# A two-block transformer layer on one core: the first norm's row, the order of the first projections, and the layout of their first weights are changed

## What is computed

```
h = rmsnorm(x, g_mix)                       # x: 256 x 1024
z = h @ w_in                                # w_in: 1024 x 2560
b_gate, c_gate, x_in, u, v = split(z)       # 512 columns each
zz   = c_gate * x_in
conv = sum(shift(zz, k) * w_conv[k] for k in range(3))
y_conv = b_gate * conv
y_sgu  = gelu(u) * (w_spatial @ layernorm(gelu(v)) + b_spatial)
x = x + concat(y_conv, y_sgu) @ w_out
x = x + moe(rmsnorm(x))                     # 32 experts, 201 MB of weights
...                                         # gate, second block
```

## Time and profile before

| | before |
|---|---|
| median of 3 runs | 949.59 us (949.17 to 949.7) |
| the profiled execution's own time | 947.69 us |
| its span | 946.0 us |
| TensorE busy in the span | 915.5 us, 97% |
| VectorE, ScalarE, GpSimd busy | 53%, 35%, 4% |
| read from HBM | 287.43 MB, 305 GB/s over the span |
| GB/s in slices 7 to 21 of 40 (142 to 497 us) | 429 to 432 |
| mean granted clock of TensorE | 0.997 |

### The profile page before, as it was taken

One profiled execution on the slowest core, in us unless ns is written; L12 is line 12 of the kernel. 1 busy time (PEld: TensorE's weight loads), 2 busy tenths in 40 slices (PEclk: granted clock), 3 DMA queues, 4 the chain that ended last, 5 costly groups with the idle time before them and its releaser, 6 DMA issues.

```text
span 946.0 us, 14147 instructions
## 1 busy us (share of the span) xinstructions
PE 915.5 (97%) x5866; PEld 647.2 (68%) x5866; DVE 503.3 (53%) x871; ACT 331.1 (35%) x531; POOL 36.7 (4%) x39
## 2 busy tenths in 40 slices
PE   7999999999999899999999989999999999999997
PEld 6997734443344434335453389989989999999886
DVE  7784612222232312123221189999999977766642
ACT  6832210100111000011000088556676755544541
POOL 1000000000000000000000000123320000000000
PEclk9999999999999999999999999999999999999999
DMA  9997799999999999999999984643424435554301
GB/s 345 400 387 311 301 389 430 430 432 430 430 429 430 429 429 430 430 430 429 432 430 421 420 382 159 250 164 142 176 93 178 179 112 198 230 196 179 134 0 45
DMA packets 28981, 289.45 MB, mean 306 GB/s; under 512 B 3056, under 2 KB 6384, under 8 KB 12400
## 3 DMA queue, kind: packets, MB, share of 16 engines
q1 hardware_dynamic: 28192, 286.91, 74.2%
q10 hardware_dynamic: 720, 1.57, 0.4%
HBM read 287.43 MB, written 1.05 MB: 305 GB/s over the span
## 4 chain that ended last, share of the span: by engine, by line
PE 76%; DVE 12%; SPq 5%; ACT 2%; issue 2%; DMA 2%; DVEq 0%; POOL 0%; ACTq 0%
PE ps L279 75%; DVE wl L275 5%; SPq L2325 5%; DMA ring<-in_w_pg 2%; DVE arena L1578 1%; ACT wh L268 1%; PE ps L1081 1%; DMA arena<-in_xT 0%; DVE arena L393 0%; DVE arena L1970 0%; DVE arena L2041 0%; ACT h_h L1449 0%; DVE arena L1486 0%; DVE mg_l L1977 0%; DVE mix_l L624 0%
## 5 line engine op out<-in xcount | busy, mean ns | idle before, releaser
L279 PE MATMUL ps<-ring,arena 128*64 128x512 f32 x1216 | 339.1, 597 | 4.9 <-issue 4.8
L275 DVE TENSOR_TENSOR wl<-ring,wh 128x1024 fp32r<-128x1024 f32 x150 | 182.1, 1247 | 38.3 <-ACT wh L268 38.1
L279 PEld LDWEIGHTS ps<-ring,arena 128*64 128x64 f32 x1216 | 108.9, 137 | 122.6 <-issue 120.9
L268 ACT ACTIVATE wh<-ring 128x1024 fp32r<-128x1024 f32 x150 | 151.9, 1052 | 46.3 <-PE ps L279 30.8
L279 PE MATMUL ps<-arena 128*64 128x512 f32 (+4 forms) x448 | 157.5, 521 | 1.1 <-DMA ring<-in_moe 0.6
L1186 DVE SCALAR_TENSOR_TENSOR arena<-ps,arena 128x512 f32<-128x512 f32 x16 | 12.0, 751 | 202.5 <-PE ps L279 202.5
L279 PEld LDWEIGHTS ps<-arena 128*64 128x64 f32 (+2 forms) x448 | 55.0, 144 | 87.5 <-issue 82.6
L279 PE MATMUL ps<-up_h,wh 128*128 128x256 f32 x352 | 85.5, 281 | 1.1 <-ACT up_h L2030 1.1
L279 PE MATMUL ps<-up_l,wh 128*128 128x256 f32 x352 | 82.1, 280 | 0.0
L1256 ACT ACTIVATE y_h<-ps 128x512 fp32r<-128x512 f32 x32 | 19.0, 596 | 151.9 <-PE ps L279 151.9
L279 PEld LDWEIGHTS ps<-up_h,wh 128*128 128x128 f32 x352 | 66.3, 188 | 1.3 <-issue 1.3
(11 more groups left out here) (283 smaller groups left out, 1460.9 us busy)
## 6 DMA issues: line engine op xcount, KB each, us to landing
ring<-in_moe SPq DMA_DIRECT2D x69, 2048.0 KB, 22.6
arena<-in_moe SPq DMA_DIRECT2D x17, 2048.0 KB, 22.6
ring<-in_w_in SPq DMA_DIRECT2D x12, 2048.0 KB, 9.6
ring<-in_w_up SPq DMA_DIRECT2D x11, 2048.0 KB, 7.9
ring<-in_moe SPq DMA_DIRECT2D x24, 512.0 KB, 15.1
ring<-in_w_dn SPq DMA_DIRECT2D x5, 2048.0 KB, 7.8
ring<-in_w_out SPq DMA_DIRECT2D x4, 2048.0 KB, 16.1
arena<-in_moe SPq DMA_DIRECT2D x8, 512.0 KB, 14.6
```

What stands on the lines that cost most here:

```text
L268: e.activation(wh(i), raw_piece(i), ACT.Copy).then_inc(*hi.up(i))
L275: e.tensor_tensor(wl(i), raw_piece(i), wh(i), SUB).then_inc(*lo.up(i))
L279: return e.matmul(o, l, r, start=first, stop=final, skip_group_check=True)
```

## The change

Five things change together, all in the first projection:

1. The order of the five weights becomes 0, 2, 1, 3, 4: the gate c comes second, v third.
2. The first weight lies in memory piece by piece, so that each of its loads reads one contiguous stretch per partition and not eight of 512 bytes.
3. The row no longer comes from squares by feature. The column `RT` is put on the diagonal of two 128x128 matrices (`DG`), and one product with a matrix of ones spreads it over all partitions. It is placed before the fourth piece of the gate, and the constants are loaded earlier for it (`cst`, which holds the identity).
4. VectorE instead of ScalarE rounds features 4 to 7 of the input. GpSimd has no squares left.
5. Everything that follows is put in an order that fits: on VectorE the gate is scaled ahead of v's mean, and v's variance moves into the convolution's loop.

```diff
-    out = [("in1", i) for i in range(5)] + [("out1", i) for i in range(2)]
+    out = [("in1", i) for i in (0, 2, 1, 3, 4)] + [("out1", i) for i in range(2)]
...
         def mixer_pe(e):
...
-            e.wait_ge(*made.at("ones"))
-            squares((1, 0, 3, 2, 5, 7, 4, 6))
             three(e, ps[3][:, 0:256], "in1", 0, 0, XGH, XGL, xg)
             for j in range(1, 4):
                 three(e, ps[3 + j][:, 0:256], "in1", 0, j, XGH, XGL)
+            for j in range(4):
+                if j == 3:
+                    e.wait_ge(*made.at("ones"))
+                    e.wait_ge(*diag.at(0))
+                    mm(e, ps[7][:, 0:256], one, DG.rearrange("p a b -> p (a b)"), True, True).then_inc(*means.up("r1"))
+                    e.wait_ge(*row.at("r"))
+                three(e, ps[CB[j]][:, 0:256], "in1", 2, j, XGH, XGL)
             for i in range(2):
+                e.wait_ge(*cgate.at(i))
                 wide(e, ps[i][:, :], "in1", 1, i, XGH, XGL)
-            for j in range(4):
-                b = CB[j]
-                if j < 2:
-                    e.wait_ge(*gelu_v.at(j))
-                elif j == 2:
-                    e.wait_ge(*roots.at("r1"))
-                three(e, ps[b][:, 0:256], "in1", 2, j, XGH, XGL)
...
         def mixer_dve(e):
...
+                if c == 4:
+                    for d in range(4, 8):
+                        e.tensor_scalar(XGH[:, d, :], XT[:, d, :], vcol("g_mix", d), None, M).then_inc(*xg_hv.up(d))
...
-            split_lo(e, 4)
-            recip(e, "r1", R1B)
-            e.wait_ge(*recips.at("r1"))
-            e.tensor_tensor(R2B, R1B, R1B, M).then_inc(*vc.up())
+            split_lo(e, 8)
+            recip(e, "rt", RT)
+            e.wait_ge(l_cst, 16)
+            e.wait_ge(*recips.at("rt"))
+            for i in range(2):
+                k = e.tensor_scalar(DG[:, i, :], ident, RT[:, i:i + 1], None, M)
+            k.then_inc(*diag.up(0))
+            e.wait_ge(*means.at("r1"))
+            e.tensor_copy(R1B, ps[7][:, 0:256]).then_inc(*row.up("r"))
+            e.wait_ge(*row.at("r"))
+            e.tensor_tensor(R2B, R1B, R1B, M).then_inc(*row.up("r2"))
             for j in range(4):
                 e.wait_ge(*proj.at("in1", 0, j))
                 e.tensor_tensor(UG[:, j, :], ps[3 + j][:, 0:256], R1B, M).then_inc(*u_.up(j))
-                split_lo(e, j + 6)
-            recip(e, "rt", RT)
-            split_lo(e, 12)
+                split_lo(e, 9 if j else 0)
+            e.wait_ge(*row.at("r2"))
+            for j in range(4):
+                e.wait_ge(*proj.at("in1", 2, j))
+                e.tensor_tensor(CR[:, j, :], ps[CB[j]][:, 0:256], R2B, M).then_inc(*cgate.up(j))
+                split_lo(e, 10 + j)
+            split_lo(e, 14)
             e.wait_ge(*gelu_v.at(1))
...
-            split_lo(e, 14)
+            split_lo(e, 16)
             for j in range(4):
...
-                split_lo(e, j + 20)
+                split_lo(e, j + 18)
             split_lo(e, 24)
...
         def mixer_act(e):
...
-            split_hi(e, 4)
+            split_hi(e, 8)
...
-            root(e, "r1", R1B, ps[2][:, 0:256])
-            split_hi(e, 8)
...
         def loads(e):
...
                 elif i == 0:
-                    dst, src = (v.rearrange("p (c n) -> p c n", c=8) for v in (dst, src))
-                    e.dma_start(dst[:, :, 0:128], src[:, :, 0:128]).then_inc(ring_sem[k], 16)
...
+                    e.dma_start(dst[:, 0:1024], src[:, 0:1024]).then_inc(ring_sem[k], 16)
...
                 if i == 1:
                     e.dma_start(XK, dr["x"]).then_inc(l_xk, 16)
+                    e.dma_start(cst[:], dr["cst"]).then_inc(l_cst, 16)
```

More of the change, by code:

```diff
@@ L178, in build @@
         FIRST = n_piece[("pgate", 0), 0]
-        P = ([("in1", 0, j) for j in range(4)] + [("in1", 1, i) for i in range(2)]
-             + [("in1", n, j) for n in (2, 3, 4) for j in range(4)]
+        P = ([("in1", n, j) for n in (0, 2) for j in range(4)] + [("in1", 1, i) for i in range(2)]
+             + [("in1", n, j) for n in (3, 4) for j in range(4)]
              + [("out1", n, i) for n in range(2) for i in range(2)]
@@ L216, in raw_piece @@
                 return w[:, j * 1024:j * 1024 + 1024]
-            if name == "pgate":
+            if name == "pgate" or (name, n) == ("in1", 0):
                 return piece_view(w[:, j * 1024:j * 1024 + 1024], name)
@@ L382, in build @@
         means = sig("means", ["r1", "r3", "r5", "r4", "mu", "var", "r6", "r7"])
-        roots = sig("roots", ["r1", "rt", "vv", "r2", "r3", "r45", "r4", "rs", "r6", "r7", "o0", "o1"])
-        recips = sig("recips", ["r1", "rt", "vv", "r2", "r3", "r45", "rs", "r4", "r7", "r6", "o0", "o1"])
+        roots = sig("roots", ["rt", "vv", "r2", "r3", "r45", "r4", "rs", "r6", "r7", "o0", "o1"])
+        recips = sig("recips", ["rt", "vv", "r2", "r3", "r45", "rs", "r4", "r7", "r6", "o0", "o1"])
         def root(e, key, dst, src, squared=0):
@@ L405, in build @@
         XK = A(2048, 2, 1024)
-        SQ0 = A(6144, 8, 256)
         WS = A(8192, 8, 256)
@@ L411, in build @@
         UG = A(o + 1024, 4, 256)
+        DG = A(o + 1792, 2, 128)
         Z = A(o + 2048, 4, 258)
@@ L427, in build @@
         made = sig("made", ["eps", "ones", "zpad", "gsq", "gpre"])
-        xg_h = sig("x_hi", range(8))
-        sq0_v, sq0_a, sq0_p = sig("sq0_v", [0, 2]), sig("squares", [4, 6]), sig("sq0_p", range(1, 8, 2))
+        xg_h, xg_hv = sig("x_hi", range(4)), sig("x_hi_v", range(4, 8))
+        diag = sig("diag", [0])
+        row = sig("row", ["r", "r2"])
         xg = sig("x_lo", range(8))
@@ L510, in mixer_pe @@
             for j in range(4):
-                e.wait_ge(*cgate.at(j))
+                e.wait_ge(*(gelu_v if j < 2 else cgate).at(j))
                 three(e, ps[CB[j]][:, 0:256], "in1", 4, j, XGH, XGL)
@@ L559, in mixer_dve @@
             e.memset(Z[:, :, 0:2], 0.0).then_inc(*made.up("zpad"))
+            e.wait_ge(l_vec, 16)
             for c in range(8):
@@ L651, in build @@
         xc = sig("xc", range(2))
-        vsq = sq0_a.then(range(2))
+        vsq = sig("squares", range(2))
         vvar = sig("vvar", [0])
@@ L691, in mixer_act @@
             e.wait_ge(l_vec, 16)
-            for c in range(8):
-                if c % 4 == 0:
-                    e.wait_ge(l_xT2 if c else l_xT, 16)
+            e.wait_ge(l_xT, 16)
+            for c in range(4):
                 e.activation(XGH[:, c, :], XT[:, c, :], ACT.Copy, scale=vcol("g_mix", c)).then_inc(*xg_h.up(c))
-                if c in (4, 6):
-                    e.activation(SQ0[:, c, :], XT[:, c, :], ACT.Square).then_inc(*sq0_a.up(c))
-            split_hi(e, 4)
+            split_hi(e, 8)
             e.wait_ge(*made.at("eps"))
-            e.wait_ge(*means.at("r1"))
-            root(e, "r1", R1B, ps[2][:, 0:256])
-            split_hi(e, 8)
             e.wait_ge(l_xk, 16)
@@ L710, in mixer_act @@
             root(e, "rt", RT, RT)
+            split_hi(e, 12)
             for j in range(4):
@@ L713, in mixer_act @@
                 e.activation(UG[:, j, :], UG[:, j, :], ACT.Gelu_apprx_tanh).then_inc(*gelu_u.up(j))
-            split_hi(e, 12)
+            split_hi(e, 16)
             e.wait_ge(*recips.at("rt"))
@@ L725, in mixer_act @@
                 e.activation(SM[:, 200:712], VG[:, i, :], ACT.Square, accum_out=VV[:, i:i + 1]).then_inc(*vsq.up(i))
+            split_hi(e, 18)
             e.wait_ge(*vvar.at(0))
@@ L762, in mixer_pool @@
         def mixer_pool(e):
-            for c in range(1, 8, 2):
-                e.wait_ge(l_xT if c < 4 else l_xT2, 16)
-                e.tensor_tensor(SQ0[:, c, :], XT[:, c, :], XT[:, c, :], M).then_inc(*sq0_p.up(c))
             e.wait_ge(l_ws, 16)
@@ L2330, in loads @@
                 elif i == 0:
[L2331 to L2334 removed]
+                    e.dma_start(dst[:, 0:1024], src[:, 0:1024]).then_inc(ring_sem[k], 16)
+                    e.dma_start(dst[:, 1024:2048], src[:, 1024:2048]).then_inc(l_second, 16)
+                    e.dma_start(dst[:, 2048:4096], src[:, 2048:4096]).then_inc(s_half, 16)
                 else:
@@ L2424, in _layout @@
     r["w_in"] = _cols(np.concatenate([w[:, 1536:2048], w[:, 2048:], w[:, 512:1024], w[:, 1024:1536], w[:, :512]], 1), 5)
+    r["w_in"][0] = r["w_in"][0].reshape(128, 8, 4, 128).transpose(0, 2, 1, 3).reshape(128, -1)
     r["w_out"] = _cols(i["w_out"][0], 2)
```

18 lines of the change are left out of this document (1 added, 17 removed).

## The result

| | before | after |
|---|---|---|
| median | 949.38 us (4 runs, 949.16 to 949.7) | 958.85 us (4 runs, 956.95 to 960.87) |
| the profiled execution's own time | 947.69 us | 958.21 us |
| its span | 946.0 us | 956.5 us |
| mean granted clock of TensorE | 0.997 | 0.991 |

The change makes the kernel slower by 1.0%: ratio 1.0102, 95% interval 1.009 to 1.0113. Forecast were 956.6 us and a range of 953.6 to 959.8, so the time is 9.5 us up where 7.0 were forecast.

The account below looks back on a forecast made before the run. The mixer's chain, paced by TensorE to 49 us and VectorE to 76, was taken to set the end through the experts' load restart. Loop 2.6 late plus stretch 3.8, rounded 6.5, plus clock 0.5: 7.0 later, 956.6 us, range 953.6 to 959.8.

Parts of the forecast that it names:

- What bounds the kernel: Mixer chain up to the experts' load restart at 114.70: each us the mixer ends later delays the end by one.
- Start of TensorE: First product with the input weights: starts at 9.5 in place of 11.94, 2.4 us earlier (bounds 1.7 to 2.5).
- Half level: First weight products: TensorE runs them at the lower clock and loses 2.15 us (bounds 0 and 2.4).
- Spread product and new waits: Ahead of the gate's fourth piece 0.95 us; waits for the scaled gate 0.4 and rests of v's weight 0.3.
- VectorE's loop: Convolution loop after v's mean and two rests: starts at 51.6 in place of 48.98, 2.6 us late.
- Inside the stretch: VectorE from the loop's start to `gated`: two more rests 2.27 and the variance 1.56, in sum 3.8 us, none covered.
- TensorE while it waits: Gap of some 4 us between mixed features, then half level clock: 0.5 us lost (bounds 0 and 1.8).
- all losses at their upper bound: Rival: first load no faster (0.7), longer half level (0.25), 1.8 for 0.5 at `out1`; 958.9 us, chance 0.13.

Follow-up runs that it names:

- e3_row: Changed kernel with the old order of the weights and VectorE's old order from the mean on, spread product between the two wide ones; 951.15 us, ratio 1.0017.
- e2_rests_early: Changed kernel with the two rests of x_in's weight moved ahead of v's mean, into VectorE's idle time; 955.65 us.
- e10_mended: Changed kernel with 13 idle products at the start, two rests ahead of v's mean and 8 idle products in the later gap; 954.92 us.
- e1_warm: Changed kernel with 13 idle TensorE products ahead of the first weights; 957.45 us.
- e4: Changed kernel with the row made from squares again, the gate still second; 955.52 us, ratio 1.0071.
- e5: Changed kernel with 8 idle products in TensorE's gap ahead of mixed feature 4; 956.98 us.
- e9_short_variance: Changed kernel with v divided by its spread in only 8 of 512 columns, so not a correct layer; 957.88 us.
- e7_conv_act: Kernel before the change with the convolution's first multiplication moved from VectorE to ScalarE; 947.83 us, ratio 0.9983.
- e8_combo: e3_row with 13 idle products at the start and the convolution's first multiplication moved from VectorE to ScalarE; 948.45 us, ratio 0.9987.
- e11_combo2: e8_combo with ScalarE's first gelu of v put ahead of the four gelus of u; 946.78 us, ratio 0.9973.

## Why the prediction was right, point by point

The direction, the size within its range and the main mechanism were right. Not every term was.

*What bounds the kernel.* Right. The last rest moved by 7.6, SyncE's restart by 8.3, and the issue of the next weight behind the experts by 9.4 (from 529.15 to 538.52). No slack in the loads took any of it.

*Start of TensorE.* The term was mis-sized: 9.5 forecast, 10.62 measured. The first piece landed at 9.5, not at 8.5. The cause is mostly that this landing moves from run to run: it was 8.5 in e3_row, 8.7 in e2_rests_early, 10.4 in e10_mended, for the same loads. Before, the squares covered it; now it is on the path. The reading behind the 8.5 was weak: the first piece before was rounded straight behind other work, so the 1.4 us between two starts of ScalarE isn't the time between two landings.

*Half level.* Right, and shown by e1_warm: the first piece lost 1.95 (forecast 2.15). The 4.3 us at half level that the forecast halves don't follow from its own 4.8, and the term isn't as fixed as its narrow place in the sum suggests: in the profiles without products ahead of the weights the first piece took from 4.43 (e2_rests_early) to 5.29 us (e3_row). The profile's granted clock reads 1.00 there all the same. The Trainium skill ("TensorE: Matmul & The Clock Gate", Part 1) warns that clock events of the trace can't be relied on one by one; the spacing of 0.21 and 0.12 is what decides.

*Spread product and new waits.* Forecast 0.95 and 0.7. From 32.42, where the product began, to 33.54 it is 1.12. The waits for the scaled gate and for the rests of v's weight read 0.17 and 0.16 in brackets, but the starts show more: the gate's fourth piece takes 3.25 us (33.54 to 36.79) and the others 2.81, the first wide product 6.10 (36.79 to 42.89) and the second 5.60. So they cost 0.44 and 0.50, in sum 0.94. x_in began at 48.49, 1.2 later than the forecast: 1.1 by the start, 0.2 by the product and 0.2 by the waits, less 0.4 in u's four pieces (13.35 us, forecast 11.6 + 2.15).

*VectorE's loop.* From x_in's beginning to the first `zx` 4.3 us were forecast (47.3 to 51.6), 4.29 measured. Forecast 2.6 late, measured 3.8, the difference being x_in's.

*Inside the stretch.* 3.8 forecast, 3.79 measured, the same to 0.02 in e4, e1, e2, e5 and e10, and gone in e3. The rows give it to the two terms of the forecast: rests 2.27 (forecast 2.27), variance 1.52 (1.56). e9_short_variance prices a third of the variance (two multiplications 0.53 shorter, the stretch 0.53 shorter); the rests were not tried one by one.

*TensorE while it waits.* Forecast a gap of some 4 us, the clock at 0.50 and a loss of 0.5 (bounds 0 and 1.8); measured 3.85, 0.50 and 0.7, and 0.5 to 1.6 in the variants.

*What is left.* 6.5 became 7.6, nearly all by x_in's place, and 0.5 became 0.7, that makes 8.3 of 9.5. That the measured 958.85 is nearly the rival's 958.9 (all losses at their upper bound) is chance: of its three terms the first load came even later than it says, the half level cost less and the gap 0.7 and not 1.8. In the trace, the stretch from SyncE's first issue at full pace (136.94 before, 145.24 now) to the gate weight's loads is 1.1 longer than before and the one from there to the end another 1.1. These have the same instructions in all kernels. In the profiles of the other kernels the first is 392.3 to 394.0 long (before 392.2) and the second 416.6 to 418.9 (before 416.8), so a us either way says little there. The spans differ by 10.5; the profiled run of before was 1.7 below its median and that of after 0.6, which leaves 9.5. What makes up the last 1.2 stays open, and no run was made for it; single runs of one kernel differ by more (before: 947.2 to 951.6).

## What to carry to other kernels

Before a product is moved earlier, ask what the next engine in the chain does between two fixed points and count its queue in program order: here VectorE's idle time lay ahead of a row that waits for v's products, and work that had been done ahead of the loop's first row (two rests and the variance) came to stand behind it. A reordering that keeps TensorE busy can thus cost the full sum of what another engine then does late. When such a stretch is shortened, look which engine sets the pace next: in e7_conv_act 2.06 us saved on VectorE gave 1.44, and in e8_combo TensorE's gain ran into ScalarE's queue. Work that looks superfluous at the start (the squares) may have been covering both the landing of the first load and TensorE's slow start; replace it only together with something that keeps the engine busy until the first weights are there.

## What the runs showed of the hardware

- In the changed kernel the granted clock in the profile's rows reads 1.00 from 10 to 16 us, while matmuls of 128x256 behind an idle start follow each other at 0.21 us up to about 15 us and then at 0.12. In the later gap it reads 0.50 (77 to 83 us), and there rows and spacing agree.
- The clock fell at different places of nearly the same gap: in the changed kernel within the first of its 3.85 idle us (0.74 over 76 to 77 us), in e2_rests_early only after work had begun again behind 3.76 us (1.00 over 77 to 78, 0.53 over 78 to 79).
- Behind thirteen products and 1.20 or 1.24 us of idle time the first piece ran at full level (2.96 us in e1_warm, 2.92 in e8_combo); behind the same products and 1.99 or 2.71 us it took 4.3 us (e10_mended, e11_combo2), with the clock at 0.50 by 13 us. In e10_mended it fell while TensorE was busy again (0.85 over 12 to 13 us). These are four runs, and no rule follows from them.
- The first 512 KB of weights, issued at 2.2 us, were there between 8.5 and 10.4 us in the nine kernels in which ScalarE waited for them.
